# Decay weights of a projection in smaller items at other places, and the loads of a mixing step in another order

## What is computed

```
p = h @ w_in                       # q_a, k_a, v_a, g_a, r_a, qkv_b, g_b, a_b, beta_b
lr = einsum('btr,zrk->zbtk', r_a, w_lr) + b_lr
gla_log_a = log_sigmoid(lr) / 16   # per direction z, token, key dim
b = cumsum(log_a)                  # in each chunk
scores = sum(q_i * k_j * exp(b_i - b_j)), j <= i
dS = (k * exp(b_last - b))^T v;  inter = (q * exp(b)) S_prev
```

## Time and profile before

| | |
|---|---|
| runs | 1657.52, 1660.69, 1659.67 us, median 1659.67 |
| profiled execution, its own time | 1664.6 us |
| its span | 1662.8 us, mean granted PE clock 0.961 |
| busy | PE 1517.3 (91%), DVE 946.6 (57%), ACT 745.6 (45%), POOL 265.5 (16%) |
| projection | about 62 to 539 us |
| mixing | 541 to 880 us |
| HBM traffic | 178.17 MB read, 74.05 MB written |

### The profile page before, as it was taken

How to read it: one execution, slowest core, us unless ns; L and a number is a source line. 1 busy time by engine, 2 the same in 40 slices (tenths; PEclk the granted TensorE clock), 3 DMA queues, 4 the chain that set the end, 5 groups by cost and what they waited for, 6 DMA issues and landing times. The chain is left out here.

```text
span 1662.8 us, 33993 instructions
## 1 busy us (share of the span) xinstructions
PE 1517.3 (91%) x14508; PEld 1284.8 (77%) x14508; DVE 946.6 (57%) x1330; ACT 745.6 (45%) x1249; POOL 265.5 (16%) x237
## 2 busy tenths in 40 slices
PE   7699999998899697787888997899999999999997
PEld 6488878786798687776777886788888878888885
DVE  4345451475540245555557439455555599988875
ACT  6446253546541444435434215455555554333333
POOL 0001110011110132233223104132222200000000
PEclk9699999998999899999899999999999999999999
DMA  9313332355984466656614311244445586454322
GB/s 325 84 62 107 89 112 63 111 178 162 290 262 143 126 209 188 196 172 206 182 52 164 115 64 63 96 139 142 156 160 164 177 310 253 141 183 161 123 89 102
DMA packets 195736, 254.44 MB, mean 153 GB/s; under 512 B 34525, under 2 KB 127201, under 8 KB 195586
## 3 DMA queue, kind: packets, MB, share of 16 engines
q1 hardware_dynamic: 190002, 234.31, 43.4%
q0 software_dynamic: 5584, 17.95, 3.4%
HBM read 178.17 MB, written 74.05 MB: 152 GB/s over the span
## 5 line engine op out<-in xcount | busy, mean ns | idle before, releaser
L87 PE MATMUL fps<-xh_m,w1r_hi 128*128 128x512 f32 x448 | 176.6, 394 | 11.9 <-ACT s L2562 3.1
L88 PE MATMUL fps<-xl_m,w1r_hi 128*128 128x512 f32 x448 | 175.5, 392 | 0.0
L89 PE MATMUL fps<-xh_m,w1r_lo 128*128 128x512 f32 x448 | 175.3, 391 | 0.0
L87 PE MATMUL fps<-bh,ah 128*128 128x512 f32 x448 | 174.4, 389 | 0.4 <-DVE acc L2891 0.4
L88 PE MATMUL fps<-bl,ah 128*128 128x512 f32 x448 | 174.3, 389 | 0.0
L89 PE MATMUL fps<-bh,al 128*128 128x512 f32 x448 | 174.3, 389 | 0.0
L80 PE MATMUL ps_main<-whi,hhi 128*128 128x256 f32 x416 | 126.8, 305 | 6.5 <-ACT t_sb L879 4.0
L2534 ACT ACTIVATE ah<-araw 128x2048 fp32r<-128x2048 f32 x28 | 53.8, 1921 | 162.6 <-PE fps L89 133.6
L80 PE MATMUL ps_main<-hhi,whi 128*128 128x512 f32 (+1 forms) x336 | 125.6, 374 | 0.0
L81 PE MATMUL ps_main<-wlo,hhi 128*128 128x256 f32 x416 | 122.8, 295 | 0.0
L82 PE MATMUL ps_main<-whi,hlo 128*128 128x256 f32 x416 | 122.7, 295 | 0.0
(11 more groups left out here) (325 smaller groups left out, 3301.0 us busy)
## 6 DMA issues: line engine op xcount, KB each, us to landing
s_hid<-hb SPq DMA_DIRECT2D x112, 256.0 KB, 2.3
araw<-s_hid SPq DMA_DIRECT2D x28, 1024.0 KB, 5.6
room<-in_w_ada SPq DMA_DIRECT2D x32, 512.0 KB, 4.9
w1raw<-in_w_ff SPq DMA_DIRECT2D x16, 1024.0 KB, 5.7
w2b<-in_w_ff SPq DMA_DIRECT2D x16, 1024.0 KB, 9.8
raw<-in_w_in SPq DMA_DIRECT2D x14, 1024.0 KB, 5.3
s_wl<-room SPq DMA_DIRECT2D x24, 512.0 KB, 4.6
wl<-s_wl SPq DMA_DIRECT2D x16, 768.0 KB, 7.2
```

Of the source, the lines that this page charges most:

```text
L87: pe.matmul(out, lhi, rhi, start=start, stop=False, skip_group_check=True)
L88: pe.matmul(out, lhi, rlo, start=False, stop=False, skip_group_check=True)
L89: return pe.matmul(out, llo, rhi, start=False, stop=stop, skip_group_check=True)
```

## The change

Rate pieces leave the list of outputs. PE makes two of them after each of ticks 3 to 8, into the three buffers `ps_sq`, ACT's passes read PSUM directly into one of two `lr_e` halves, and DVE does its prefix sums there. Context comes first (`LRSEG`). Each part keeps its prefix sums in a buffer of its own (`cs_of`). Items hold two token tiles: 33, of 1024 elements per partition, in two slots, from the twelfth use on in three. The first three stand at ticks 6 to 8, the others at 10 + 8*i//5. The late weights use other rooms, and their first loads wait for the rates to be done. In mixing, the row vectors come ahead of the keys, the level weights are loaded in their own step in three pieces (levels 0 to 2, 3, 4 and 5) behind waits on PE's solves and updates, `out_weight` and `token_keys` come before the keys, and the keys wait for the first scores.

```diff
-        cs_lat, cs_ctx = room[:, 5120:7200], m.sb("cs_ctx", [P, 1040])[:]
-        slots = [room[:, 7200 + 2048 * i:9248 + 2048 * i] for i in range(2)]
+        cs_ctx = m.sb("cs_ctx", [P, 1040])[:]
+        cs_of = [room[:, 5120:7200], room[:, 7200:9280], cs_ctx]
+        slots = [room[:, x:x + 1024] for x in (9280, 10304, 0)]
...
-        late = [room[:, x:x + KT * P] for x in (0, KT * P, 4 * KT * P)]
+        late = [cs_ctx[:, :KT * P], lr_e[:].rearrange("p x n -> p (x n)"), room[:, 4 * KT * P:5 * KT * P]]
...
-        ITEMS = [(0, kind) for kind in KINDS] + [(2, KIN)] + [(1, kind) for kind in KINDS]
-        starts = [1 + 2 * i for i in range(9)] + [20 + 2 * i for i in range(8)]
+        ITEMS = ([(CTX, KIN), (0, KIN), (1, KIN)] + [(x, kind) for x in (0, 1) for kind in REST]
+                 + [(x, kind) for x in (2, 3) for kind in [KIN] + REST])
+        SLOT = [i % 2 if i < 12 else i % 3 for i in range(len(ITEMS))]
+        starts = [6, 7, 8] + [10 + 8 * i // 5 for i in range(len(ITEMS) - 3)]
+        SUMS_AT = {n: i for i, n in enumerate(starts)}
+        WEIGH_AT = {n + 1: i for i, n in enumerate(starts)}
+        def rates_at(n):
+            return (2 * n - 6, 2 * n - 5) if 3 <= n < 9 else ()
...
             def load_late(g):
                 if g < NL:
-                    sp.wait_ge(wt_done, 8 if g < 2 else 9)
-                    sp.wait_ge(st_qk, 16)
+                    sp.wait_ge(wt_done, 1)
+                    sp.wait_ge(lr_done, 12)
+                    sp.wait_ge(rate_out, 2)
...
+            def rates(j):
+                n, b = SEG[LRSEG[j // 4]][1], j % 2
+                act.wait_ge(lr_ready, j + 1)
+                if j >= 2:
+                    act.wait_ge(lr_done, j - 1)
+                act.activation(lr_e[:, b, :n], ps_sq[:, j % 3, :n], ACT.Abs).then_inc(lr_abs, 1)
...
+            def rates(j):
+                if j >= 3:
+                    pe.wait_ge(lr_done, j - 2)
+                t0, n = SEG[LRSEG[j // 4]]
+                pe.matmul(ps_sq[:, j % 3, :n], wlr[:, j % 4 * P:(j % 4 + 1) * P], raT[0:RANK + 1, t0:t0 + n], start=True,
+                          stop=True).then_inc(lr_ready, 1)
...
+            def weights(s, lo, hi):
+                n = s - TC
+                after(sp, sc_ready, 2 * n - (1 if hi <= 3 else 0))
+                sp.dma_start(wl[:, lo:hi], S["wl"][n, :, lo:hi]).then_inc(ld_wl[0 if hi <= 3 else 1], 16)
...
             def step(p, r):
                 if p is not None:
+                    if lat(p):
+                        sp.wait_ge(tr_ready, 2 * r + 1)
+                        weights(p, 0, 3)
                     if p + 1 < NT:
                         decays(p + 1)
+                    if lat(p):
+                        sp.wait_ge(ds_ready, 2 * r + 1)
+                        weights(p, 3, 4)
                     if p:
                         values(p)
+                    if p < KT:
+                        out_weight(p)
+                    if lat(p):
+                        sp.wait_ge(tr_ready, 2 * r + 2)
+                        weights(p, 4, 6)
+                    if p:
+                        token_keys(p)
                     if p + 1 < NT:
+                        if lat(p):
+                            sp.wait_ge(sc_ready, 2 * (p - TC) + 1)
                         keys(p + 1)
```

More of the change, by code:

```diff
@@ L585, in item @@
             t0, n = PART[part]
[L586 removed]
+            cs = cs_of[2 if part == CTX else part // 2]
+            off, z = (0, 8 * PW) if part == CTX else (8 * PW * (part % 2), 16 * PW)
+            return t0, n, kind, slots[SLOT[i]], cs, off, z
         def view(t, off, dims):
@@ L672, in _ @@
                 sp.wait_ge(st_g[i], 32)
-            for i in range(2):
-                sp.wait_ge(st_w[i], 32 * ((len(ITEMS) + 1 - i) // 2))
+            for i in range(3):
+                sp.wait_ge(st_w[i], 32 * SLOT.count(i))
         @block.gpsimd
@@ L894, in _ @@
                     if (u, j) == (VA + 1, 4):
[L895 to L900, removed]
+                        for x in (2, 0, 1):
+                            chunk_rates(x)
+                n = tick(u, kind, j, s)
+                for x in rates_at(n):
+                    rates(x)
+                if n in SUMS_AT:
+                    weight_exp(SUMS_AT[n])
                 if u >= 1 and i + 1 == out_by[u - 1] + 1 and u + 1 < NU:
@@ L1009, in weight_sums @@
-            def weight_sums(i):
[L1010 to L1014, removed]
+            def rates(j):
+                x = LRSEG[j // 4]
+                n, cs = SEG[x][1] // P, cs_of[x]
+                if j == 0:
+                    for b in range(2):
+                        dve.wait_ge(st_n[b], 4 * 16 + 2 * 16)
+                    dve.memset(view(room[:, 5120:9280], 0, [[PW, 64]]), 0.0).then_inc(pad_done, 1)
+                    dve.memset(view(cs_ctx, 0, [[PW, 16]]), 0.0).then_inc(pad_done, 1)
+                    dve.wait_ge(pad_done, 2)
+                    dve.wait_ge(init_done, 4)
+                dve.wait_ge(lr_ln, j + 1)
+                z, a = j % 4 // 2, j % 2
+                by_chunk = lambda x, c: x.rearrange("p (t c j) -> p t c j", t=n, c=2)[:, :, c]
+                for c in range(2):
+                    last = dve.scalar_tensor_tensor(view(cs, PW * (4 * n * z + 2 * a + c) + 1, [[4 * PW, n], [1, C]]),
+                                                    by_chunk(ps_sq[:, j % 3, :n * P], c), 0.0, by_chunk(lr_e[:, j % 2, :n * P], c),
+                                                    ALU.min, ALU.subtract)
+                last.then_inc(lr_done, 1)
+                if j % 4 == 3:
+                    dve.wait_ge(lr_done, j + 1)
+                    for x in range(4 * n):
+                        at = slice(2 * PW * x, 2 * PW * (x + 1))
+                        last = dve.tensor_tensor_scan(cs[:, at], restart[:], cs[:, at], 0.0, ALU.mult, ALU.add)
+                    last.then_inc(cs_done, 1)
@@ L1085, in _ @@
                     token_scales()
-                if (u, j) in WEIGH_AT and kind != "lr":
-                    weigh(WEIGH_AT[(u, j)])
-                if (u, j) in SUMS_AT and kind != "lr":
-                    weight_sums(SUMS_AT[(u, j)])
+                n = tick(u, kind, j, s)
+                for x in rates_at(n):
+                    rates(x)
+                if n in WEIGH_AT:
+                    weigh(WEIGH_AT[n])
+                if n in SUMS_AT:
+                    weight_sums(SUMS_AT[n])
                 if kind == "gate":
@@ L1228, in _ @@
                         turn(cn - 2, (0, 1) if s < last_s else (2,))
+                    for x in rates_at(tick(u, kind, j, s)):
+                        rates(x)
             late_turn(NLATE - 1)
```

191 lines of the change are left out of this document (78 added, 113 removed).

## The result

Six runs of the changed kernel gave 1669.62 us as median (1666.52 to 1675.39), six of the kernel before on the same chip 1660.18 (1654.74 to 1661.18). The ratio is **1.0078, with a 95% interval from 1.0046 to 1.0110**: about 13 us slower, where I had forecast some 20 us faster. The profiled execution took 1666.52 us, with a span of 1664.7 and a mean granted clock of 0.956.

What follows compares the result with a forecast made beforehand. A serial item chain was taken to lose PE most of 34.0 us in V and gate tiles. Span: 1662.8 - 19 (projection) - 0.8 (mixing) = 1643 us; allowing for a profiled run 4.9 above the median, 1640 us, range 1628 to 1652.

Steps and rivals of the forecast that it cites:

- What bounds the kernel: Projection's V and gate tiles: 34.0 us lost, 21.4 as PE idle and 12.6 at lower clock, behind a serial item chain.
- (1), smaller items: V tiles: two-tile items cycle in about 3.8 us against 4.6 us available, so the item chain stops binding them.
- (2), rates in ticks 3 to 8: V tiles: ScalarE's queue takes 37 us between copies of tiles 6 and 9; PE waits 6, about 2 more at tick 15.
- Rival B: V tiles, ticks 6 to 12: the queue holds PE twice as long, only 9 us less, 1650; chance 0.10.
- (3), gates: Gate tiles: ScalarE needs 75.9 of 104.0 us, so is not the bound; no steady stall; the 3.5 us DMA wait goes.
- Rival C: Gates: ScalarE becomes the bound, 37 us lost there in place of 2 to 3, time 1674; chance 0.05.
- The 47 us for drains: Gates: the skill's drain figure would add some 47 us to ScalarE's 76 over 35 table loads, time near 1660.
- My 2 us at the first gates: Start of the gate tiles: 2 us of stall allowed there, with no stall in steady state after.
- (4), slots and stores: Projection items: three slots and half-size stores cost zero, since a slot is wanted some four ticks after its product.
- rival E: Items do not flow: a slot, store or late load holds VectorE, all gain is lost, 1659; chance 0.03.
- (5), mixing: Mixing stage: earlier row vectors save 0.8 us; moved loads cost 0, with bounds of -13 and +13 for contention.
- rival A: Mixing gives part back: load bursts in the middle of the step starve PE, +13 us, 1653; chance 0.14.

Runs made afterwards that it cites:

- the repaired projection: Changed projection with before's mixing, plus three slots from the first item and stores ahead of weight loads, late loads between stores: 0.9900 and, repeated, 0.9898 of before.
- The third slot alone: Changed projection with before's mixing, plus a third slot from the first item on, SyncE's order unaltered: 1655.47 us, 0.9946 of before.
- the order alone: Changed projection with before's mixing and its own slots; only SyncE's order altered, stores ahead of weight loads, late loads between stores: 1652.10 us, 0.9954 of before.
- the loads made once: Level weights loaded for the first latent step only: with pieces and waits in their own step, 0.9989 of before; in the kernel before, 0.9982.

## Why the prediction was wrong, point by point

**What bounds the kernel**, right in the main: of the 34 us lost in the V and gate tiles, the repaired projection got back 20 against the profile of before (259.4 us in place of 279.4) and 18 against the mean of the seven with before's projection; I had said 19. The timed runs of it are 17 us faster than before (0.9900 and 0.9898). About half of the 20 are PE's stops (24.0 us in the stage, now 14.5) and half its busy time (255.4 us, now 244.9), near the 11 and 8 that my sum has for the two.

**(1), smaller items**, right in its mechanism: a 256-wide subtraction measured 0.42 us alone and 0.34 from the next (347.22, then 347.57 and 347.90), against my 0.35. The V tiles stop being bound by the chain once slots are free: PE is busy for 64.00 of 64.00 us.

**(2), rates in ticks 3 to 8**, right: ScalarE's queue from the copy of tile 6 to that of tile 9 took 329.51 - 294.32 = 35.2 us (worked out: 37), PE's wait at the end of it 4.5 us (said: 6). Rival B would have needed twice that.

**(3), gates**, right: in the repaired kernel the last 27 intervals take 517.26 - 412.38 = 104.9 us, 3.88 each, and ScalarE is busy for 68.62 of 105.00. Rival C is refuted. 30 table loads of 1.28 us are in those 68.62. The Trainium skill ("ScalarE: Activation LUTs", What ACT_TABLE_LOAD costs) adds 1.38 us of drain to each. By an estimate from that figure ScalarE would have needed 68.6 + 30*1.38 = 110 us, more than the 105.00, and this is not what the kernel shows. (The 47 us for drains in my forecast are of 34 loads, not 35.) My 2 us at the first gates were too few: the first late column waits 4.2 to 5.3 us for its weights in the seven profiles with the new projection, a DMA wait that I had struck out. The last gate's copy is at 517.26 where I had said about 518; in the changed kernel it is at 533.64.

**(4), slots and stores: this is the step that failed.** I wrote that "The cover is a free slot: a store is issued in the tick of its product and the slot is wanted some four ticks later", and costed it at zero. Neither half holds. For the first fourteen items there are two slots, and the slot is wanted after two ticks in most cases; and SyncE issues in its own order, so of the three stores that were missed one left behind a weight load and landed in 9.3 us, and two left 3.6 and 3.9 us after their products and landed in 8.8 and 7.8. With the 3.5 us of the repaired kernel and no such delay each would have landed before its slot was wanted, if only just (341.5 against 341.63, 371.8 against 374.43, 388.0 against 388.14). I had even given the price right behind it, "a DMA landing, a few us each": the three waits are 5.6, 6.2 and 8.0 us, 19.8 in all. That this is near the 19 that I had forecast as gain is chance, since it is VectorE that waits: PE itself stood 11.3 us of it (0.6 with the third slot, 0.3 with the order). The rest of the 18 us between the two projections (277.1 and 259.4) is 2.5 us less standing at the gates and 3.7 us less busy time. A row that I had quoted spoke against me: in the earlier trace rows VectorE already stood 5.4 us for the stores of its items before, with two slots of which each was wanted again three ticks after its product, where now it is mostly two. It was rival E ("The items do not flow"), to which I gave 0.03, with "Against: three slots".

**(5), mixing**, wrong by its size: I took 0 between -13 and +13. The changed mixing measured +6.0 us (1.0036), its level weights alone +9.6 (1.0058). I had named the mechanism (loads where PE is dense) and rival A's price of 13, but thought neither end nearer. It may be that the burst stood where PE was waiting for other things too, and that the pieces fall among dense work. This is argued, not shown: in the 7.2 us behind the loads of before PE was busy for 56.0 of 65.8 us (85%), in the 6 us behind each piece for 108.7 of 124.4 (87%). Two fears were void: the keys behind the new order cost nothing (0.9995), and level weights never released the scores. The row vectors do come earlier, and ScalarE's first exponentials start 7.3 us into the stage in place of 8.4. But the gain of 0.8 us was not seen, since the keys now come behind them: PE waits 5.4 us for their load (`PE pd L1750 <- DMA kc<-s_k`), for which it didn't wait before, and the first solve comes 37.1 us into the stage, 36.5 before.

Together: the gain of 19 missed and 6 lost in mixing give 6 us slower than before; 13 were measured. The changed projection by itself is 5 us slower (1.0032, interval 1.5 to 9 us), and its profile doesn't show where: its projection lasts 277.1 us, in the midst of the seven with before's. This part stays open.

## What to carry to other kernels

If items are made smaller and more frequent, count the slot again: how many there are at each stage of the program, when each is wanted next, and what stands ahead of its store in the queue that issues it. An issue order is a queue like an engine's; a store behind a 1 MB load or behind a wait for another engine has that as its price. And spreading a load does not make it cheap: here the same bytes in three pieces within their own step cost 0.6% more than in a burst at the end of the step before. What it is about their place is open, so a new place for a load has to be timed, with the load left out as a control.

## What the runs showed of the hardware that I had not expected

The stores of `s_qin`, 256 KB each, took 7.1 us from issue to landing (median of four) behind the weight loads of the changed kernel, and 3.5 us in the repaired one, where they leave ahead of them. The third slot alone left them at 7.2, the order alone brought 3.5. (Issues of DMAs between 320 and 400 us, first the changed kernel, then the repaired one.)

```profile
s_qin<-room SPq DMA_DIRECT2D x4, 256.0 KB, 7.1
```

```profile
s_qin<-room SPq DMA_DIRECT2D x4, 256.0 KB, 3.5
```

The stops of PE without a releaser seem to become shorter when other loads are taken away, from 33 to 27 us in the means; one of the seven profiles with all loads has 28.2 too. One of 3.37 us, with the level weights in their own step:

```profile
794.93 1.47 PE L1770 MATMUL pr<-st,kc 128*64 128x128 f32 x12 [3.37 <-issue]
```

In the stretch of that stop the DMA engines are busy throughout, and two packets of the instruction queues are among them (packets, MB, share):

```profile
q1 hardware_dynamic: 582, 1.06, 96.3%
q8 instruction: 1, 0.02, 2.2%
q14 instruction: 1, 0.01, 0.6%
```

Of the stops of 1.4 us and more, 7 of 11 before and 9 of 11 here have such a packet within or up to 1 us ahead of them. That the engine waits for its instructions, and these for the data's DMAs, fits this and the two runs with the loads made once. In three more profiles (both with the loads made once, and the second of the repaired kernel) it is 16 of 19, so 32 of 41 in all, where of 240 stretches of 3 us set evenly over the stage 130 have such a packet (60 packets in 332.3 us before). So it is more than chance, but what holds what is not shown. The Trainium skill ("Runtime: NRT & Kernel Launch", Instruction fetch mechanics) gives blocks of 16 KiB, and 0.98 MB in 60 packets agree with it. Its "mostly hidden" would not hold for this stage if the reading is right.
